# Expert weights in two column groups of 2048 and 1536, kept in a byte ring, in a decoder trunk

## The chip, the cores and the metric

One core of one Trainium2 chip runs the program. The metric is the device time of one execution in microseconds (us); lower is better. All inputs and outputs lie in HBM in float32.

## The reference, cut to what matters

Two decoder layers over 256 tokens of width 1024. Each has a token mixer, a cross attention into 256 memory tokens and a feed-forward part. The feed-forward part of the first layer is dense; that of the second routes each token to 2 of 8 experts:

```
logits = hf @ w_router                       # 256 x 8
topv, topi = top_k(logits, 2); wts = softmax(topv)
gate = sum over the two of one_hot(topi) * wts
for e in range(8):
    out += gate[:, e:e+1] * ((silu(hf @ wg[e]) * (hf @ wu[e])) @ wd[e])
```

wg[e] and wu[e] are 1024 x 3584, wd[e] is 3584 x 1024, so one expert has 44.04 MB of weights. A final RMSNorm follows.

## The kernel before, in words

**Two parts.** The trunk (both mixers, both attentions, the dense feed-forward) streams weights in units of 1 MB through six raw buffers, splits them into two float32r parts on ScalarE and VectorE and multiplies three times. The change does not touch that work, only where its buffers lie. The experts come last, on a plain float32 path: weights go from HBM to a slot and straight into TensorE as the moving operand.

**Visits.** Each expert is visited once (further visits would follow if an expert had more tokens than slots, which the code decides at run time; here there are eight visits). A visit holds up to 96 slots of tokens, as three groups (h) of 32; visits 1, 4 and 7 (LIGHT) take two groups, 64 slots. The gather (L1613) brings the visit's tokens into `he` by products with a selection matrix S. Gate and up products (gate_up, L1626) use 32 slot columns of `he` as the stationary operand and 256 weight columns as the moving one. Four column groups of the array (q = 0 to 3) work side by side, each on another quarter of the unit's columns and on another 32 partitions of PSUM. ScalarE applies silu (L868), VectorE multiplies with up (act_rows, L1253), TensorE transposes the result (act_t_, L1647), ScalarE copies it to SBUF as `aT` (L880), and the down products (L1660) sum into PSUM banks 4 and 5 over the whole visit. In the next visit the sum is evacuated by y_hi and y_lo (L855, L1227) and added to the tokens by the scatter (L1680, two products for each of four pieces) and add_piece (L1241). ST_AFTER places the slot products (L1705), which turn S into the rows that the next scatter needs; VectorE's slot_rows (L1248) copies them.

**Units.** The 3584 columns are four groups of 1024, 1024, 1024 and 512. A gate or up unit is 256 rows of one group: 2 rows of 4 KB to a partition. In the last group, gate and up share four units ("both"), each loaded by two DMAs of 512 KB with runs of 2 KB. A down unit is 256 rows of wd, again 2 rows of 4 KB to a partition. A visit has 42 units of 1 MB (BODY). Their order (`order`, L297 to L316) is gate, up, and then the down products of the group before.

**Slots.** The units go round 21 slots of 8 KB per partition (MR, L247), which lie over buffers that the trunk has finished with. The first 21 loads wait for the trunk to leave each place (L429 to L449); after that a load waits until the unit 21 places earlier is used (slot_wait, L418). All loads are issued by SyncE, in order, on one queue.

**PSUM.** Gate has banks 0 and 1, up 2 and 3, the down sums 4 and 5; scatter, slot products and transposes share 6 and 7. Where TensorE changes between products on 32 columns of the array and products on 128 (transposes, scatter, slot products, gather), T_AFTER, SCATTER_AFTER and ST_AFTER (L322 to L324) say after which unit.

Of the kernel before, what the change touches and what calls it, by code (L numbers as in the profile page):

```python
# [20 lines left out]
F32 = mybir.dt.float32  # L21
# [6 lines left out]
P = 128  # L28
# [4 lines left out]
MR = 21  # L33
# [14 lines left out]
def trunk(nc, a, out):  # L48
# [10 lines left out]
    NJ = DFE // C  # L59
    BODY = 6 * NJ  # L60
# [8 lines left out]
    assert NT == 2 and KD == 8 and NG == 4 and DEPTH == 2 and FH % P == 0 and BODY % MR == 0  # L69
# [63 lines left out]
    raw = [place(f"raw{i}", [P, UNIT], F32) for i in range(RAW)]  # L133
    whi = [place(f"whi{i}", [P, UNIT], F32R) for i in range(SPL)]
    wlo = [place(f"wlo{i}", [P, UNIT], F32R) for i in range(SPL)]
    x = place("x_res", [P, NT, D], F32)
    Ah = place("a_hi", [P, KD, SEQ], F32R)
    Al = place("a_lo", [P, KD, SEQ], F32R)
    Bh = place("b_hi", [P, KD, SEQ], F32R)
    Bl = place("b_lo", [P, KD, SEQ], F32R)  # L140
# [3 lines left out]
    vv = place("v_tok", [P, NT, D], F32)  # L144
    moe_top = at["top"]
    gT = place("gatesT", [P, 2 * KD, SEQ], F32)
    sc = at["top"]
    at["top"] += 32768
    ident = place("ident", [P, P], F32)
# [38 lines left out]
    hg = place("h_tok", [P, NT, D], F32, sc + 8192)  # L188
    m0 = moe_top + 8192

    def moe(name, shape, dt, region):
# [14 lines left out]
    silu_t = moe("silu_tmp", [P, SG * 256], F32, work)  # L206
    act_t = moe("act_tok", [P, SG * 256], F32, work)
# [34 lines left out]
    aT = [place("actT", [P, 2 * SG, P], F32, place_of["mem_lo"]), place("actT_end", [P, 2 * SG, P], F32, place_of["mem_lo"] + 4096)]  # L242
    gfin = place("g_final_rows", [P, D], F32, moe_top)

    SPLITS = [place_of[f"{w}{(U0 - SPL + i) % SPL}"] for i in range(SPL) for w in ("whi", "wlo")]
    RAWS = [place_of[f"raw{(U0 + i) % RAW}"] for i in range(RAW)]
    slots = [moe_top, place_of["b_hi"], place_of["b_lo"], sc + 24576] + RAWS[:4] + [  # L247
        place_of["kT"], place_of["v_tok"], sc + 16384] + RAWS[4:] + SPLITS + [place_of["a_lo"], sc]
    assert len(slots) == MR
    slot_t = [place(f"slot{i}", [P, UNIT], F32, where) for i, where in enumerate(slots)]  # L250

    def moe_raw(i):
        return slot_t[i % MR][:]
# [11 lines left out]
    with contextlib.ExitStack() as ctx:  # L265
# [4 lines left out]
        moe_loaded = [ctx.enter_context(nc.semaphore(f"moe_loaded{i}")) for i in range(MR)]  # L270
# [26 lines left out]
        GROUPS = [(j, min(2, NJ - j)) for j in range(0, NJ, 2)]  # L297
        GATE, UP, DOWN, order = [0] * len(GROUPS), [0] * len(GROUPS), [0] * len(GROUPS), []

        def add_group(w, g, first):  # L300
            first[g] = len(order)
            for part in range(2 * GROUPS[g][1]):
                order.append((w, g, part))

        for g in range(len(GROUPS)):
            if GROUPS[g][1] == 2:
                add_group("gate", g, GATE)
                add_group("up", g, UP)
            else:
                GATE[g] = UP[g] = len(order)  # L310
                for part in range(4):
                    order.append(("both", g, part))
            if g:
                add_group("down", g - 1, DOWN)
        add_group("down", len(GROUPS) - 1, DOWN)
        assert len(order) == BODY  # L316

        GATE_END = [GATE[g] + 4 for g in range(len(GROUPS))]
        UP_END = [UP[g] + 4 for g in range(len(GROUPS))]  # L320
        LOADS = [32 if w == "both" else 16 for w, _, _ in order]
# [3 lines left out]
        NG4 = len(GROUPS)  # L325
# [9 lines left out]
        def landed(i, v):  # L335

            m = i % MR
            return every(v, LOADS[m] + LOADS[m + MR], LOADS[i] + (LOADS[m] if i >= MR else 0))

        def y_piece(g, q):  # L340

            return ps[q * QP:(q + 1) * QP, 4:6, :].rearrange("p a b -> p (a b)")[:, g * 256:(g + 1) * 256]
# [9 lines left out]
        with nc.Block() as block:  # L352
# [3 lines left out]
            def _(sp):  # L356
# [39 lines left out]
                def load_expert_unit(i, e):  # L396
                    t = moe_raw(i)
                    w, g, part = order[i]
                    j, n = GROUPS[g]
                    if w == "both":  # L400
                        k = 2 * part
                        dst = t.rearrange("p (k h n) -> p k h n", k=2, h=2)
                        for h, name in enumerate(("w_e_gate", "w_e_up")):
                            src = a[name][0][bass.ds(e, 1), k * P:(k + 2) * P, j * C:(j + 1) * C]
                            sp.dma_start(dst[:, :, h, :], src.rearrange("e (k p) n -> p (e k) n", p=P)
                                         ).then_inc(moe_loaded[i % MR], 16)
                        return
                    if w == "down":
                        k, kk = 4 * j + 2 * part, 2
                        src = a["w_e_down"][0][bass.ds(e, 1), k * P:(k + kk) * P, :]  # L410
                    else:
                        kk = 2
                        k = kk * part
                        src = a["w_e_" + w][0][bass.ds(e, 1), k * P:(k + kk) * P, j * C:(j + n) * C]
                    dst = t.rearrange("p (k n) -> p k n", k=kk)
                    sp.dma_start(dst, src.rearrange("e (k p) n -> p (e k) n", p=P)).then_inc(moe_loaded[i % MR], 16)

                def slot_wait(i, v):  # L418

                    n = i - MR  # L420
                    sp.wait_ge(s["unit_used"], every(v, BODY, U0 + n + 1))

                def load(e, v):
                    for i in range(BODY):
                        slot_wait(i, v)
                        load_expert_unit(i, e)

                for i in range(MR):  # L429
                    if i == 1:  # L430

                        sp.wait_ge(s["unit_used"], mix_start[-1])
                    elif 4 <= i < 8:

                        sp.wait_ge(s["lo_ready"], U0 - RAW + i - 4 + 1)
                    elif i == 8:

                        sp.wait_ge(s["scores_done"], NH * DEPTH)
                    elif i == 9:

                        sp.wait_ge(s["o_done"], NH * DEPTH)
                    elif 11 <= i < 7 + RAW:
                        sp.wait_ge(s["lo_ready"], U0 - RAW + i - 7 + 1)
                    elif 7 + RAW <= i < 7 + RAW + 2 * SPL:
                        sp.wait_ge(s["unit_used"], U0 - SPL + (i - 7 - RAW) // 2 + 1)
# [1381 lines left out]
```

## Time and profile before

| | |
|---|---|
| median of 3 runs | 1585.14 us (1584.75 to 1585.96) |
| the profiled execution, its own time | 1584.88 us |
| its span, first to last instruction | 1583.2 us |
| granted TensorE clock, mean | 0.997 of full speed |
| busy: TensorE, VectorE, ScalarE | 99%, 32%, 26% |
| read from HBM | 475.61 MB |
| first product of the experts | 720.45 us into the span |
| first and last visit begin | 720.45 and 1487.18 us |

Engines are PE (TensorE matmul), PEld (its weight loads), DVE (VectorE), ACT (ScalarE), SPq (SyncE's queue). Times of a timeline are microseconds from the first instruction; "x192" counts instructions; a bracket gives the idle time of the engine before the row and what ended it, where "issue" is time in which it waited for nothing that the profile shows.
### The profile page before, as it was taken

What the parts mean: (1) busy time and instruction counts of PE and PEld (TensorE: products, weight loads), DVE (VectorE), ACT (ScalarE), POOL (GpSimd) and SP (SyncE); (2) the same over time, 40 slices, a digit from 0 to 9 for tenths busy, and PEclk for the clock granted to TensorE, in tenths of its full rate; (3) what the DMA queues carried; (4) which work ended last, traced back from release to release, by engine and by line L of the source; (5) the groups of instructions that cost most, each with busy time, mean ns of one, the idle gap of its engine ahead of it and who ended that gap; (6) DMA issues with size and microseconds to landing.
All of it is one profiled execution on the core that took longest, in us unless ns stands there. A gap on an engine that the chain in (4) does not pass through costs nothing. (4 is left out here: it accounts for less than half of the span.)

```text
span 1583.2 us, 42366 instructions
## 1 busy us (share of the span) xinstructions
PE 1564.0 (99%) x19703; PEld 1186.4 (75%) x19703; DVE 498.8 (32%) x563; ACT 412.2 (26%) x502; POOL 33.5 (2%) x119
## 2 busy tenths in 40 slices
PE   8999999999999999999999999999999999999996
PEld 8999898998989998986656566666565656655654
DVE  5554656455456646543002010020020100100202
ACT  5444464443445444531001010010010100100102
POOL 1000000000000000103000000000000000000000
PEclk9999999999999999999999999999999999999998
DMA  9655643556466555778999999999999999999995
GB/s 352 189 183 171 213 160 121 168 179 205 160 209 187 182 180 190 283 282 310 372 395 362 402 408 404 405 408 398 408 408 388 407 408 391 407 403 396 408 391 219
DMA packets 164693, 479.41 MB, mean 303 GB/s; under 512 B 9028, under 2 KB 14244, under 8 KB 164516
## 3 DMA queue, kind: packets, MB, share of 16 engines
q1 hardware_dynamic: 164516, 476.69, 80.7%
q8 instruction: 155, 2.54, 0.7%
q14 instruction: 22, 0.18, 0.0%
HBM read 475.61 MB, written 1.05 MB: 301 GB/s over the span
## 5 line engine op out<-in xcount | busy, mean ns | idle before, releaser
L1642 PE MATMUL ps<-slot,h_slots 128*32 128x256 f32 x9408 | 523.7, 380 | 0.0
L1642 PEld LDWEIGHTS ps<-slot,h_slots 128*32 128x32 f32 x9408 | 299.8, 110 | 205.3 <-issue 13.0
L930 DVE TENSOR_TENSOR wlo<-raw,whi 128x2048 fp32r<-128x2048 f32 (+1 forms) x116 | 259.0, 2236 | 208.1 <-ACT whi L602 208.1
L1337 PE MATMUL ps<-a_hi,whi 128*128 128x256 f32 x992 | 281.4, 284 | 0.0
L1337 PE MATMUL ps<-a_hi,wlo 128*128 128x256 f32 x992 | 280.7, 283 | 0.0
L1337 PE MATMUL ps<-a_lo,whi 128*128 128x256 f32 x992 | 280.7, 283 | 0.0
L602 ACT ACTIVATE whi<-raw 128x2048 fp32r<-128x2048 f32 (+1 forms) x116 | 216.7, 1869 | 162.9 <-PE ps L1337 104.6
L1674 PE MATMUL ps<-slot,actT 128*32 128x256 f32 x4032 | 223.6, 379 | 0.0
L1674 PEld LDWEIGHTS ps<-slot,actT 128*32 128x32 f32 x4032 | 130.2, 110 | 86.5 <-issue 1.3
L1337 PEld LDWEIGHTS ps<-a_lo,whi 128*128 128x128 f32 x992 | 190.4, 192 | 0.1
L1337 PEld LDWEIGHTS ps<-a_hi,whi 128*128 128x128 f32 x992 | 190.4, 192 | 0.1
L1337 PEld LDWEIGHTS ps<-a_hi,wlo 128*128 128x128 f32 x992 | 190.4, 192 | 0.0
L1260 DVE TENSOR_TENSOR act_tok<-silu_tmp,ps 128x768 f32<-128x768 f32 (+3 forms) x32 | 27.4, 856 | 493.5 <-PE ps L1642 341.9
L602 ACT ACTIVATE actT<-ps 128x768 f32<-128x768 f32 (+1 forms) x24 | 17.5, 731 | 565.4 <-PE ps L1657 565.4
L1246 DVE TENSOR_TENSOR x_res<-x_res,ps 128x512 f32<-128x512 f32 x32 | 21.3, 686 | 96.7 <-PE ps L1684 96.7
L1357 PE MATMUL ps<-whi,a_hi 128*128 128x512 f32 x128 | 50.7, 396 | 1.1 <-DVE a_lo L935 1.1
L1357 PE MATMUL ps<-wlo,a_hi 128*128 128x512 f32 x128 | 49.9, 389 | 0.0
L1357 PE MATMUL ps<-whi,a_lo 128*128 128x512 f32 x128 | 49.8, 389 | 0.0
L877 ACT ACTIVATE silu_tmp<-ps 128x768 f32<-128x768 f32 (+3 forms) x32 | 23.2, 726 | 74.9 <-PE ps L1642 74.9
L1674 PE MATMUL ps<-slot,actT_end 128*32 128x256 f32 x672 | 38.1, 380 | 0.6 <-DMA slot<-in_w_e_down 0.6
L1337 PE MATMUL ps<-mem_hi,whi 128*128 128x256 f32 x128 | 36.5, 285 | 0.0
L1337 PE MATMUL ps<-b_hi,whi 128*128 128x256 f32 x128 | 36.2, 283 | 0.0
(245 smaller groups left out, 1361.3 us busy)
## 6 DMA issues: line engine op xcount, KB each, us to landing
slot<-in_w_e_down SPq DMA_DIRECT2D x112, 1024.0 KB, 17.9
slot<-in_w_e_gate SPq DMA_DIRECT2D x96, 1024.0 KB, 18.6
slot<-in_w_e_up SPq DMA_DIRECT2D x96, 1024.0 KB, 18.7
raw<-in_w_in SPq DMA_DIRECT2D x32, 1024.0 KB, 5.5
slot<-in_w_e_gate SPq DMA_DIRECT2D x32, 512.0 KB, 8.5
slot<-in_w_e_up SPq DMA_DIRECT2D x32, 512.0 KB, 12.0
raw<-in_w_xk SPq DMA_DIRECT2D x8, 1024.0 KB, 5.2
raw<-in_w_xv SPq DMA_DIRECT2D x8, 1024.0 KB, 5.2
```

The lines of the kernel that those rows point to most:

```text
L602: return act.activation(dst, src, ACT.Copy, scale=scale)
L877: act.activation(silu_t[to, 0:w], ps[of, 0:2, :].rearrange("p a b -> p (a b)")[:, 0:w], ACT.Silu).then_inc(s["silu_ready"], 1)
L930: dve.tensor_tensor(wlo[n % SPL][:, 0:size], raw[n % RAW][:, 0:size], whi[n % SPL][:, 0:size].bitcast(F32), ALU.subtract).then_inc(s["lo_r ...
L1246: dve.tensor_tensor(xs, xs, bank(6 + n % 2), ALU.add).then_inc(s["xadd_done"], 1)
L1260: dve.tensor_tensor(act_t[of, 0:w], silu_t[of, 0:w], ps[of, b0:b0 + 2, :].rearrange("p a b -> p (a b)")[:, 0:w], ALU.mult).then_inc(s["act ...
L1337: ins = pe.matmul(o[:, d, :], w[wi][:, k, d * P:(d + 1) * P], xs[xi][:, k0 + k, :], start=first and d % 2 == 0, stop=last, skip_group_chec ...
L1357: ins = pe.matmul(o[:, t, 0:nn], xs[xi][:, k0 + k, t * P:(t + 1) * P], w[wi][:, k, :], start=j == 0 and k == 0 and n == 0, stop=j == n_uni ...
L1642: ins = pe.matmul(o[q * QP:(q + 1) * QP, h * n:(h + 1) * n], he[:, kt, h * QP:(h + 1) * QP], w[:, k, q * n:(q + 1) * n], start=kt == 0 and ...
L1674: ins = pe.matmul(o[q * QP:(q + 1) * QP, h * 256:(h + 1) * 256], lhs, w[:, k, q * 256:(q + 1) * 256], start=g == 0 and f == 0 and h % 2 == ...
```

## The change

- The 3584 columns become **two groups** of 2048 and 1536 (WIDE = 512 and 384 columns for each of the four column groups of the array). A product takes 512 or 384 weight columns.
- A gate or up unit is one k-tile of 128 rows: one run of 8 KB (1 MB in all) or 6 KB (768 KB) for a partition. A down unit has two consecutive rows to a partition (8 KB, 1 MB) in the first group and three (12 KB, 1.5 MB) in the second. A visit has 44 units: 28 of 1 MB or more and 16 of 768 KB.
- Since partition p of a down unit now holds consecutive rows of wd, the activations are permuted to match: silu reads PSUM as "(c b) -> b c" and writes `act_t`, and VectorE multiplies in place with the same order.
- The slots become a **ring of 168 KB** per partition in two halves, 22 units each (TURN); a load waits for the last unit of the other half that its bytes cover.
- PSUM: gate has banks 0 to 2, up 3 to 5, the down sums 6 and 7. Transposes use the up banks, the gather banks 3 and 4, the slot products bank 5, the scatter 3, 4, 6 and 7.
- Order of a visit on TensorE: 8 gate, 8 up, 4 gate of group 1, 2 down, 4 gate, 8 up, 6 down, 4 down. The scatter follows unit 2 in one stretch, the slot products unit 7, the transposes units 17 and 35, the gather unit 42.

```diff
-    slots = [moe_top, place_of["b_hi"], place_of["b_lo"], sc + 24576] + RAWS[:4] + [
-        place_of["kT"], place_of["v_tok"], sc + 16384] + RAWS[4:] + SPLITS + [place_of["a_lo"], sc]
+    order = []
+    order += [("gate", 0, k) for k in range(KD)] + [("up", 0, k) for k in range(KD)]
+    order += [("gate", 1, k) for k in range(4)] + [("down", 0, k) for k in range(2)]
+    TURN = len(order)
+    order += [("gate", 1, k) for k in range(4, KD)] + [("up", 1, k) for k in range(KD)]
+    order += [("down", 0, k) for k in range(2, 8)] + [("down", 1, k) for k in range(4)]
+    BODY = len(order)
...
+    def words(i):
+
+        w, g, _ = order[i]
+        return (2 * D, WIDE[1] // P * D)[g] if w == "down" else 4 * WIDE[g]
...
+    def covered(i):
+
+        other = range(TURN, BODY) if i < TURN else range(TURN)
+        return max(n for n in other if span[n][0] < span[i][1])
...
-        T_AFTER = [GATE[g + 1] + 3 for g in range(len(GROUPS) - 2)] + [GATE[-1] + 1, DOWN[-1] - 2]
-        SCATTER_AFTER = (GATE[0] + 3, GATE[0] + 3, UP[0] + 1, UP[0] + 2)
-        ST_AFTER = GATE[1] + 1
+        T_AFTER = (end_of("up", 0) + 1, end_of("up", 1) + 1)
+        SCATTER_AFTER, SCATTER_BANKS = 2, (3, 4, 6, 7)
+        ST_AFTER = first_of("up", 0) - 1
+        GATHER_AFTER = BODY - 2
...
+                    if w == "down":
+                        r, n = WIDE[g] // P, words(i) // D
+                        q, part = divmod(k, r // n)
+                        r0 = 4 * WIDE[0] * g + q * WIDE[g]
+                        src = a["w_e_down"][0][bass.ds(e, 1), r0:r0 + WIDE[g], :].rearrange("e (p r) n -> p (e r) n", r=r)
+                        src = src[:, part * n:(part + 1) * n, :]
...
+                        src = a["w_e_" + w][0][bass.ds(e, 1), k * P:(k + 1) * P, c0:c0 + 4 * WIDE[g]].rearrange("e p n -> p e n")
...
+                def ring_wait(i, v):
+
+                    n = covered(i) - (BODY if i < TURN else 0)
+                    sp.wait_ge(s["unit_used"], every(v, BODY, U0 + n + 1))
...
-                    elif i == MR - 1:
-
-                        sp.wait_ge(s["hg_ready"], NT)
...
+                    elif block == 20:
+                        sp.wait_ge(s["unit_used"], U0)
...
-                    act.activation(silu_t[to, 0:w], ps[of, 0:2, :].rearrange("p a b -> p (a b)")[:, 0:w], ACT.Silu
+                    act.activation(act_t[:, 0:n_groups * n].rearrange("p (h b c) -> p h b c", h=n_groups, c=P),
+                                   ps[:, 0:n_groups, 0:n].rearrange("p h (c b) -> p h b c", c=P), ACT.Silu
                                    ).then_inc(s["silu_ready"], 1)
...
-                dve.memset(ps[:, 4:6, :], 0.0)
-                dve.memset(ST[:].bitcast(F32), 0.0).then_inc(s["zero_done"], 1)
+                dve.memset(ST[:].bitcast(F32), 0.0)
...
+                    rows_ = act_t[:, 0:n_groups * n].rearrange("p (h b c) -> p h b c", h=n_groups, c=P)
+                    dve.tensor_tensor(rows_, rows_, ps[:, 3:3 + n_groups, 0:n].rearrange("p h (c b) -> p h b c", c=P),
                                       ALU.mult).then_inc(s["act_ready"], 1)
...
+                dve.memset(ps[:, 6:8, :], 0.0).then_inc(s["zero_done"], 1)
                 gathered(0)
...
+                    if k == 0 and w_name == "gate" and g:
+                        pe.wait_ge(s["silu_ready"], every(v, NG2, g))
+                    elif k == 0 and w_name == "up" and g == 0:
                         pe.wait_ge(s["xadd_done"], every(v, 4, 4))
                         pe.wait_ge(s["st_ready"], every(v, 1, 1))
+                    elif k == 0 and w_name == "up":
+                        pe.wait_ge(s["actT_ready"], every(v, NG2, g))
...
+                    for h in range(n_groups):
+                        for q in range(4):
+                            ins = pe.matmul(ps[q * QP:(q + 1) * QP, b0 + h, 0:n], he[:, k, h * QP:(h + 1) * QP],
+                                            w[:, q * n:(q + 1) * n], start=k == 0, stop=k == KD - 1, skip_group_check=True)
...
+                def scatter(v):
+
+                    pe.wait_ge(s["he1_ready"], every(v, 1, 1))
+                    pe.wait_ge(s["y_ready"], every(v, 2, 2))
+                    for n, b in enumerate(SCATTER_BANKS):
...
                     for i in range(BODY):
                         (down if order[i][0] == "down" else gate_up)(i, v, n_groups)
-                        for n in range(4):
-                            if i == SCATTER_AFTER[n]:
...
+                        if i == SCATTER_AFTER:
+                            scatter(v)
                         if i == ST_AFTER:
...
+                            slot_t(v)
```

## Rows read from the trace of the kernel before

**Rows 1.** The page: its span, and TensorE's and VectorE's busy time

```profile
span 1583.2 us, 42366 instructions
PE 1564.0 (99%) x19703; PEld 1186.4 (75%) x19703; DVE 498.8 (32%) x563; ACT 412.2 (26%) x502; POOL 33.5 (2%) x119
```

**Rows 2.** The waits, 700 to 1583 us: total, times, longest; all that name TensorE and DMA

```profile
PE ps L1674 <- DMA slot<-in_w_e_down: 0.6, 1, 0.6
```

**Rows 3.** Timeline of TensorE's weight loads, visit 0 and the start of visit 1

```profile
720.45 10.09 PEld L1642 LDWEIGHTS ps<-slot,h_slots 128*32 128x32 f32 x192
...
750.07 4.91 PEld L1642 LDWEIGHTS ps<-slot,h_slots 128*32 128x32 f32 x96
755.39 0.64 PEld L1657 LDWEIGHTS ps<-ident,act_tok 128*128 128x128 f32 x6 [0.41 <-issue]
756.19 10.09 PEld L1642 LDWEIGHTS ps<-slot,h_slots 128*32 128x32 f32 x192 [0.17 <-issue]
766.36 10.27 PEld L1674 LDWEIGHTS ps<-slot,actT 128*32 128x32 f32 x192
776.72 10.27 PEld L1642 LDWEIGHTS ps<-slot,h_slots 128*32 128x32 f32 x192
...
840.44 6.82 PEld L1642 LDWEIGHTS ps<-slot,h_slots 128*32 128x32 f32 x128
847.67 0.19 PEld L1684 LDWEIGHTS ps<-y_hi,sel_slot 128*128 128x128 f32 x1 [0.41 <-issue]
...
848.79 3.18 PEld L1642 LDWEIGHTS ps<-slot,h_slots 128*32 128x32 f32 x64 [0.37 <-issue]
852.38 0.19 PEld L1684 LDWEIGHTS ps<-y_hi,sel_slot 128*128 128x128 f32 x1 [0.41 <-issue]
...
853.05 1.45 PEld L1642 LDWEIGHTS ps<-slot,h_slots 128*32 128x32 f32 x32 [0.36 <-issue]
```

**Rows 4.** The weight queue, 860 to 1560 us: packets, MB, share of 16 engines

```profile
q1 hardware_dynamic: 80246, 279.98, 101.4%
```

**Rows 5.** The same queue, 1330 to 1410 us (80 us, 4 KB runs alone)

```profile
q1 hardware_dynamic: 8408, 32.41, 101.6%
```

**Rows 6.** The same queue, 1202 to 1208 us (6 us, 2 KB runs among them)

```profile
q1 hardware_dynamic: 725, 1.84, 92.0%
```

**Rows 7.** Timeline of TensorE's weight loads in the last visit

```profile
1508.35 3.18 PEld L1642 LDWEIGHTS ps<-slot,h_slots 128*32 128x32 f32 x64
1511.94 0.42 PEld L1657 LDWEIGHTS ps<-ident,act_tok 128*128 128x128 f32 x4 [0.41 <-issue]
1512.52 6.63 PEld L1642 LDWEIGHTS ps<-slot,h_slots 128*32 128x32 f32 x128 [0.17 <-issue]
...
1565.57 1.48 PEld L1674 LDWEIGHTS ps<-slot,actT_end 128*32 128x32 f32 x32 [1.01 <-issue]
```

**Rows 8.** Timeline of VectorE after the slot products of visit 0

```profile
750.18 0.42 DVE L1250 CAST sel_slot<-ps 128x256 fp32r<-128x256 f32 x1 [4.90 <-PE ps L1712]
750.52 0.15 DVE L1251 COPY gate_slot<-ps 128x1 f32<-128x1 f32 x1
```

**Rows 9.** Timeline of VectorE as y is evacuated at the start of visit 1

```profile
840.90 2.61 DVE L1233 COPY y_slots<-ps 32x256 f32<-32x256 f32 x6 [4.79 <-PE ps L1674]
843.99 1.41 DVE L1238 SCALAR_TENSOR_TENSOR y_lo<-y_slots,gate_slot,y_hi 96x512 fp32r<-96x512 f32 x2 [0.48 <-ACT y_hi L602]
```

**Rows 10.** Groups by shape, 700 to 1583 us: busy, mean ns, idle before, releaser

```profile
L1260 DVE TENSOR_TENSOR act_tok<-silu_tmp,ps 128x768 f32<-128x768 f32 x15 | 14.3, 955 | 244.5 <-PE ps L1642 244.5
L602 ACT ACTIVATE actT<-ps 128x768 f32<-128x768 f32 x15 | 12.2, 811 | 401.2 <-PE ps L1657 401.2
L1260 DVE TENSOR_TENSOR act_tok<-silu_tmp,ps 128x512 f32<-128x512 f32 x9 | 6.2, 688 | 97.4 <-PE ps L1642 97.4
```

**Rows 11.** The weight queue in the trunk, 300 to 400 us (100 us)

```profile
q1 hardware_dynamic: 10209, 18.73, 58.0%
```

More of the change, by code:

```diff
@@ L58, in trunk @@
     C = 512
-    NJ = DFE // C
-    BODY = 6 * NJ
+    WIDE = (512, 384)
     OVER = ROUNDS * NE
@@ L143, in trunk @@
     kT = place("kT", [P, KD, SEQ], F32)
-    vv = place("v_tok", [P, NT, D], F32)
     moe_top = at["top"]
     gT = place("gatesT", [P, 2 * KD, SEQ], F32)
+    Bh = place("b_hi", [P, KD, SEQ], F32R)
+    Bl = place("b_lo", [P, KD, SEQ], F32R)
+    for u in range(U0 - RAW, U0 - 2):
+        raw[u % RAW] = place(f"raw{u % RAW}", [P, UNIT], F32)
     sc = at["top"]
     at["top"] += 32768
+    vv = place("v_tok", [P, NT, D], F32)
+    for u in range(U0 - 2, U0):
+        raw[u % RAW] = place(f"raw{u % RAW}", [P, UNIT], F32)
+    for u in range(U0 - SPL, U0):
+        whi[u % SPL] = place(f"whi{u % SPL}", [P, UNIT], F32R)
+        wlo[u % SPL] = place(f"wlo{u % SPL}", [P, UNIT], F32R)
+    Al = place("a_lo", [P, KD, SEQ], F32R)
+    ring, ring_end = moe_top + 8192, at["top"]
     ident = place("ident", [P, P], F32)
@@ L241, in trunk, with first_of, end_of @@
     yl = place("y_lo", [P, D], F32R, place_of["mem_hi"] + 4096)
[L242 to L246, printed above, removed]
-    slots = [moe_top, place_of["b_hi"], place_of["b_lo"], sc + 24576] + RAWS[:4] + [
-        place_of["kT"], place_of["v_tok"], sc + 16384] + RAWS[4:] + SPLITS + [place_of["a_lo"], sc]
[L249 to L253, printed above, removed]
+    aT = [place("actT", [P, SG * WIDE[0] // P, P], F32, place_of["mem_lo"]),
+          place("actT_end", [P, SG * WIDE[1] // P, P], F32, m0)]
+    gfin = place("g_final_rows", [P, D], F32, ring)
+    order = []
[5 more added lines that the diff above has]
+    BODY = len(order)
+    def first_of(w, g):
+        return order.index((w, g, 0))
+    def end_of(w, g):
+        return max(i for i, o in enumerate(order) if o[:2] == (w, g)) + 1
+    def words(i):
+        w, g, _ = order[i]
+        return (2 * D, WIDE[1] // P * D)[g] if w == "down" else 4 * WIDE[g]
+    span, unit_t = [], []
+    for i in range(BODY):
+        b0 = 0 if i in (0, TURN) else span[-1][1]
+        span.append((b0, b0 + 4 * words(i)))
+        assert ring + span[-1][1] <= ring_end
+        unit_t.append(place(f"unit{i}", [P, words(i)], F32, ring + b0))
+    assert span[TURN - 1][1] == span[-1][1] == ring_end - ring
+    def covered(i):
+        other = range(TURN, BODY) if i < TURN else range(TURN)
+        return max(n for n in other if span[n][0] < span[i][1])
     names = """const_loaded mem_loaded mem_t1_loaded x_loaded wpg_loaded wrt_loaded gbc_loaded setup_done
@@ L295, in cols @@
             return ap[:, :, c * C:(c + 1) * C]
[L297 to L321, printed above, removed]
-        T_AFTER = [GATE[g + 1] + 3 for g in range(len(GROUPS) - 2)] + [GATE[-1] + 1, DOWN[-1] - 2]
-        SCATTER_AFTER = (GATE[0] + 3, GATE[0] + 3, UP[0] + 1, UP[0] + 2)
-        ST_AFTER = GATE[1] + 1
-        NG4 = len(GROUPS)
+        NG2 = len(WIDE)
+        T_AFTER = (end_of("up", 0) + 1, end_of("up", 1) + 1)
+        SCATTER_AFTER, SCATTER_BANKS = 2, (3, 4, 6, 7)
+        ST_AFTER = first_of("up", 0) - 1
+        GATHER_AFTER = BODY - 2
         def every(v, per, n):
@@ L1634, in gate_up @@
[L1634 to L1644 removed]
+                    w_name, g, k = order[i]
```

229 lines of the change are left out of this document (89 added, 140 removed).

## The prediction

> **What bounds the kernel now.** I read the page first. TensorE is busy in 99% of the span and no other engine in more than 32% [rows 1], which says little by itself, since ends of matmuls are modelled. The list of waits says more: over the whole expert stage, from 720.45 us on, TensorE is seen waiting for a transfer once, for 0.6 us [rows 2]. The timeline of its weight loads then gives the rate. 192 loads run from 766.36 to 776.72, so one record (half of a product of the source, which is two records) costs 53.96 ns, or 215.8 ns for the four column groups that run together [rows 3]. At the granted full clock that is 518 cycles for 256 columns. If a record streams two cycles to a column, 512 of them are streaming and 2.5 ns are left for each four.
>
> With that rate the whole first visit closes: 2016 records (108.8 us), four rounds of transposes, three interruptions by the scatter, one by the slot products, one gather; it lasts from 720.45 to 840.44 [rows 3]. So **TensorE paces the stage**. The visits with two groups of slots issue 1344 records.
>
> The transfers are close behind. From 860 to 1560 the weight queue moved 279.98 MB, 400 GB/s [rows 4]; in a stretch of 4 KB runs it moves 405 [rows 5], and where the 2 KB runs of the last column group pass, 307 [rows 6]. Only the end shows the tie: the last unit found TensorE idle for 1.01 us [rows 7], the one place where the stock of loaded units had run out.
>
> **The change, part by part.** All prices are per visit, for a visit of three groups of slots (five) and of two (three).
>
> *Wide products.* The gate and up products go from 256 columns to 512 and 384. Columns streamed stay the same. Records fall from 1344 to 768 (896 to 512), so 144 (96) fewer groups of four, at 2.5 ns each: **-0.36 (-0.24) us**. The page "TensorEngine Tiling (Array Packing)" of the Trainium skill, section "Instruction Overhead", gives about 60 cycles of overhead to each matmul; at the full clock that is an estimate of 25 ns on each of the 4032 records removed, 101 us in all, against 2.5 us by the row. The row decides here; the other is a rival below.
>
> *Transposes.* A round of six costs what 750.07 to 756.19 holds beyond 96 records: 6.12 - 5.18 = 0.94 us [rows 3]. A round of four costs 4.17 - 3.45 = 0.72, from 1508.35 to 1512.52 [rows 7]. That is 0.28 for switching and 0.11 for each. Now four rounds (3.76; 2.88). After: two rounds, 12 and 9 transposes (8 and 6): 1.60 + 1.27 = 2.87 (1.16 + 0.94 = 2.10). **-0.89 (-0.78).**
>
> *Scatter.* One piece between products costs 4.26 - 3.45 = 0.81 us (848.79 to 853.05); the stretch of two pieces is 1.12 long where that of one is 0.67 [rows 3], so another piece adds 0.45. Three interruptions become one of four pieces: 2 x (0.81 - 0.45) = **-0.72**.
>
> *A wait is added.* The slot products now stand right before the first up product, which waits for VectorE to have copied their result, because they share a bank. Before, TensorE resumed at 750.07 and VectorE finished only at 750.52 + 0.15 [rows 3, 8]. Allowing 0.1 for the restart, the bubble is 0.70: **+0.70**. Everything on TensorE queues behind it. It can't be below zero, and above I allow 1.5.
>
> *The earlier scatter.* It waits for the evacuated y after three units instead of four. After a full visit, y was complete at 843.99 + 1.41 = 845.40, that is 4.96 after the first load of 840.44 [rows 3, 9]. Three new units take 7.7 us with three groups, but 48 x 107.3 ns = 5.15 with two, plus 0.1 of draining. Nothing is paid, with 0.3 us to spare in three visits; if y is late the price is the lateness, three times.
>
> *Activations.* VectorE's product over 768 elements takes 955 ns and over 512 takes 688 [rows 10], so 1536 elements take 1.75 us. It must be over before the transposes two units later, 3.87 us (2.58) after the last up product. ScalarE's copy grows the same way, 811 ns at 768 to 1.45, beside the next two gate units. The permuted read (a stride of 16 bytes) is nowhere in this trace: its bounds are no cost and twice the time (3.4 us). Both fit in the cover, the second barely, so I take nothing. If the cover fails, the transposes wait, and everything behind them. Silu reads under eight up units and cannot matter.
>
> *Setup.* The clearing of the y banks moves behind the rank products on VectorE (0.9 us, while VectorE awaits the gather), and the last ring slot no longer waits for the token rows. The first unit starts when it did: nothing.
>
> Sum: -0.36 - 0.89 - 0.72 + 0.70 = -1.27 in a full visit, -0.24 - 0.78 - 0.72 + 0.70 = -1.04 in a light one. 5 x 1.27 + 3 x 1.04 = 9.5, and the 1.0 us idle at the end goes too if transfers keep up: **-10.5 us**.
>
> *Do they keep up?* The last unit would have to land about 11.5 us sooner: its three rows take 2.6 us of products, and TensorE is 9 to 10 ahead. 279.98 MB in 688.5 us is 407 GB/s [rows 4]. Flat 4 KB runs give 405 [rows 5]; the short fall of 0.4% is about 3 us. The new runs are 6 to 12 KB. A packet took 1300 us / 8408 = 155 ns at a mean of 3855 B [rows 5] and 928 / 10209 = 91 ns at 1835 B [rows 11]; drawn on, 8 KB would take 292 ns, 449 GB/s. So the supply lies between 405 and 449 if longer runs do no harm. I take 415; anything over 407 gives the same time. The ring holds as much as before (21 MB), and releases at most one unit later.
>
> The profiled execution took 1584.88, its span 1583.2; less 10.5 is 1574.4, and since it stood 0.26 below the median of the runs shown, **1574.5** for the median.
>
> **The rivals.**
>
> *Transfers take over mildly (0.12).* If runs are cut at 4 KB, or 6 KB ones into 4 and 2, the supply stays at 402 to 405: 3 to 8 us of the gain are lost, 1577 to 1582. Against: the mean is now pulled down by 2 KB runs, which vanish.
>
> *Transfers take over badly; slower (0.13).* Sixteen of the 44 loads, 28.6% of the bytes, are 768 KB instead of 1 MB. The only smaller loads now, 512 KB each, are where the rate sinks to 307 [rows 6]. The Trainium skill speaks against such units: "DMA: Bandwidth & Descriptors", section "Rules for kernel authors", wants at least 1 MiB per DMA for full bandwidth. In rows: if these bytes move at r and the rest at 405, the mean falls under today's 400 from r = 388 down. At r = 350, about halfway to the 2 KB stretch, the mean is 388, 280 MB take 722 us instead of 700, and the time is about 1605. Against: those 512 KB loads also had 2 KB runs and came in pairs, which explains the dip as well. A run's start stride of 16 KB in the down weights could do the same.
>
> *The waits take it back (0.09).* If the bubble is 1.5 us, y is 1 us late in the light visits, and the strided reads overrun their cover by 0.5 in each visit, that is 6.4 + 3 + 4 = 13 us: about 1588. It decides from 1.3 us of extra waiting per visit. With half of it, 1581.
>
> *Records carry more overhead than the rate shows (0.04).* At 25 ns for each of 4032 records TensorE would save 101 us, but supply would bind at once: 280 MB at 415 GB/s takes 675 us where it took 700, so 1560 at best. Against: 215.8 ns leave no room for it.
>
> **How the numbers follow.** My own case has 0.62 and spans 1571 to 1577 (bubble 0.4 to 1.2, rounds 20% off). The range 1570.5 to 1583.5 takes in the mild transfer case and half of the waits' case and leaves out the bad transfer case, the rest of the waits and the overhead case, some 0.2. This kernel's measurement tells 0.2%, 3 us, from no change. Faster by more than that (below 1582): 0.62 + 0.11 + 0.04 + 0.02 = 0.79; within: 0.07; slower: 0.14.
>
> **What the changed profile would show.** Right: weight loads 107 ns apart (mean) in the first group and 80.6 in the second; two rounds of transposes with 12 and 9; one scatter of four pieces; an idle of TensorE's loads of 0.6 to 0.8 us after each slot stretch, released by VectorE's gate_slot; full visits of 118.7 us and light ones of 82; GB/s that falls below the cap in full visits, because the ring is full; no wait for a transfer. Wrong: waits for slots behind DMA in several visits (transfers bind), VectorE's act_tok over 3 us, or records that differ from 107 and 80.6 ns.

## The result, and the profile after

The changed kernel takes 1574.33 us (median of 4 runs, 1573.99 to 1574.77), the kernel before 1584.95 beside it on the same chip: a ratio of 0.9933 (95% interval 0.9922 to 0.9945), 10.6 us less. The prediction was 1574.5.

The page of the kernel after; its first lines answer to [rows 1], and the packets and MB of the instruction queue, before 155 and 2.54, matter further down:

```profile
span 1572.9 us, 34011 instructions
PE 1550.6 (99%) x15650; PEld 1070.5 (68%) x15650; DVE 492.3 (31%) x547; ACT 404.7 (26%) x470; POOL 33.3 (2%) x119
...
q8 instruction: 123, 2.02, 0.5%
```

The list of waits has no transfer for TensorE at all (before, one of 0.6 us [rows 2]). The timeline of TensorE's weight loads, visit 0 and what follows, answers to [rows 3]:

```profile
720.39 0.16 PEld L1630 LDWEIGHTS ps<-unit,h_slots 128*32 128x32 f32 x8
720.84 0.13 PEld L1630 LDWEIGHTS ps<-unit,h_slots 128*32 128x32 f32 x4 [0.30 <-issue]
721.27 0.13 PEld L1630 LDWEIGHTS ps<-unit,h_slots 128*32 128x32 f32 x4 [0.30 <-issue]
...
728.25 0.19 PEld L1668 LDWEIGHTS ps<-y_hi,sel_slot 128*128 128x128 f32 x1 [0.84 <-issue]
...
730.29 0.16 PEld L1630 LDWEIGHTS ps<-unit,h_slots 128*32 128x32 f32 x8 [0.35 <-issue]
...
743.30 0.20 PEld L1676 LDWEIGHTS ps<-ident,sel_tok 128*128 128x128 f32 x2 [0.84 <-issue]
743.47 0.53 PEld L1678 LDWEIGHTS ps<-gate_of_visit,sel_tok 128*128 128x128 f32 x4
744.68 0.19 PEld L1630 LDWEIGHTS ps<-unit,h_slots 128*32 128x32 f32 x8 [0.68 <-issue]
...
769.32 1.29 PEld L1639 LDWEIGHTS ps<-ident,act_tok 128*128 128x128 f32 x12 [0.62 <-issue]
770.78 0.16 PEld L1630 LDWEIGHTS ps<-unit,h_slots 128*32 128x32 f32 x8 [0.17 <-issue]
...
808.37 0.96 PEld L1639 LDWEIGHTS ps<-ident,act_tok 128*128 128x128 f32 x9 [0.41 <-issue]
809.50 10.09 PEld L1655 LDWEIGHTS ps<-unit,actT 128*32 128x32 f32 x192 [0.17 <-issue]
...
839.12 0.35 PEld L1630 LDWEIGHTS ps<-unit,h_slots 128*32 128x32 f32 x8
...
844.59 0.19 PEld L1668 LDWEIGHTS ps<-y_hi,sel_slot 128*128 128x128 f32 x1 [0.84 <-issue]
...
921.12 0.34 PEld L1630 LDWEIGHTS ps<-unit,h_slots 128*32 128x32 f32 x8
...
1546.52 10.27 PEld L1655 LDWEIGHTS ps<-unit,actT_end 128*32 128x32 f32 x192
```

Read it from the top. Loads come in fours, 0.43 us apart: the array holds four column groups at work, and the next four wait for 512 columns to pass. The idle of 0.30 before each four costs nothing, since loading overlaps the products. Visit 0 lasts from 720.39 to 839.12, 118.73 us, where it lasted 119.99; the light visit 1 from 839.12 to 921.12, 82.00, where it lasted 83.03 (840.44 to 923.47). Five times 1.26 and three times 1.03 make 9.4 us. The last row is one unbroken run of 192 loads, where before TensorE had idled 1.01 us for its last unit [rows 7]. Together 10.4 us, beside the 10.3 by which the span is shorter.

VectorE after the slot products and at the next visit's start ([rows 8, 9]):

```profile
744.12 0.42 DVE L1238 CAST sel_slot<-ps 128x256 fp32r<-128x256 f32 x1 [12.62 <-PE ps L1678]
744.46 0.15 DVE L1239 COPY gate_slot<-ps 128x1 f32<-128x1 f32 x1
...
839.58 2.61 DVE L1221 COPY y_slots<-ps 32x256 f32<-32x256 f32 x6 [3.50 <-PE ps L1655]
842.67 1.41 DVE L1226 SCALAR_TENSOR_TENSOR y_lo<-y_slots,gate_slot,y_hi 96x512 fp32r<-96x512 f32 x2 [0.49 <-ACT y_hi L597]
```

The second row ends at 744.61, and TensorE loads for its first up product at 744.68: this is the added wait. The last row ends at 844.08, 0.5 us ahead of the scatter at 844.59, so the earlier scatter waits for nothing even in a light visit.

Groups by shape for the activations ([rows 10]):

```profile
L1247 DVE TENSOR_TENSOR act_tok<-act_tok,ps 128x1536 f32<-128x1536 f32 x5 | 8.8, 1755 | 104.8 <-PE ps L1630 104.8
L870 ACT ACTIVATE act_tok<-ps 128x1536 f32<-128x1536 f32 x5 | 7.3, 1452 | 95.7 <-PE ps L1630 95.7
L597 ACT ACTIVATE actT<-ps 128x1536 f32<-128x1536 f32 x5 | 7.3, 1451 | 129.9 <-PE ps L1639 129.9
```

Silu reads PSUM in steps of 16 bytes and takes 1452 ns; ScalarE's copy of as many elements reads it in order and takes 1451.

The weight queue, 860 to 1540 us and then 980 to 1080 (packets, MB, share of 16 engines), answers to [rows 4, 5]:

```profile
q1 hardware_dynamic: 40248, 280.93, 100.1%
q1 hardware_dynamic: 6002, 41.74, 100.6%
```

413 GB/s over the whole stretch, 417 in the second, where the queue was busy throughout. In the first stretch 4477 of the packets have under 512 bytes; the others have 7.8 KB on average, as the runs of 6, 8 and 12 KB of a visit have (44.04 MB in 5632 runs). In the second stretch the trace has packets of 6144, 8192 and 12288 bytes and, besides them, only some of 4 bytes, so the runs pass whole.

### The profile page after: what moved, and what is told of

Same layout as the page of the kernel before. It is cut to its first block and busy times, and to the rows that moved or that the text cites. A ratio compares the mean times of both kernels' runs of the same rounds, so it can differ in the third digit from the quotient of the medians.

```text
span 1572.9 us, 34011 instructions
## 1 busy us (share of the span) xinstructions
PE 1550.6 (99%) x15650; PEld 1070.5 (68%) x15650; DVE 492.3 (31%) x547; ACT 404.7 (26%) x470; POOL 33.3 (2%) x119
## 3 DMA queue, kind: packets, MB, share of 16 engines
q8 instruction: 123, 2.02, 0.5%
## 5 line engine op out<-in xcount | busy, mean ns | idle before, releaser
L1630 PE MATMUL ps<-unit,h_slots 128*32 128x384 f32 (+1 forms) x5376 | 513.1, 539 | 5.0 <-issue 5.0
L1630 PEld LDWEIGHTS ps<-unit,h_slots 128*32 128x32 f32 x5376 | 183.4, 110 | 312.9 <-issue 310.4
L1655 PE MATMUL ps<-unit,actT 128*32 128x256 f32 x2688 | 149.6, 379 | 0.0
L1247 DVE TENSOR_TENSOR act_tok<-act_tok,ps 128x1536 f32<-128x1536 f32 (+3 forms) x16 | 22.1, 1380 | 396.5 <-PE ps L1630 396.5
L1655 PEld LDWEIGHTS ps<-unit,actT 128*32 128x32 f32 x2688 | 86.5, 110 | 61.1 <-issue 7.5
L1655 PE MATMUL ps<-unit,actT_end 128*32 128x256 f32 x2016 | 111.7, 379 | 0.0
L1655 PEld LDWEIGHTS ps<-unit,actT_end 128*32 128x32 f32 x2016 | 64.8, 110 | 42.9
L870 ACT ACTIVATE act_tok<-ps 128x1536 f32<-128x1536 f32 (+3 forms) x16 | 18.4, 1151 | 241.0 <-PE ps L1630 241.0
L597 ACT ACTIVATE actT<-ps 128x1536 f32<-128x1536 f32 (+1 forms) x8 | 10.3, 1291 | 183.3 <-PE ps L1639 183.3
L597 ACT ACTIVATE actT_end<-ps 128x1152 f32<-128x1152 f32 (+1 forms) x8 | 8.1, 1012 | 144.4 <-PE ps L1639 144.4
```

What stands on the lines that cost most here:

```text
L597: return act.activation(dst, src, ACT.Copy, scale=scale)
L870: act.activation(act_t[:, 0:n_groups * n].rearrange("p (h b c) -> p h b c", h=n_groups, c=P), ps[:, 0:n_groups, 0:n].rearrange("p h (c b) ...
L1247: dve.tensor_tensor(rows_, rows_, ps[:, 3:3 + n_groups, 0:n].rearrange("p h (c b) -> p h b c", c=P), ALU.mult).then_inc(s["act_ready"], 1)
L1630: ins = pe.matmul(ps[q * QP:(q + 1) * QP, b0 + h, 0:n], he[:, k, h * QP:(h + 1) * QP], w[:, q * n:(q + 1) * n], start=k == 0, stop=k == KD ...
L1655: ins = pe.matmul(o[q * QP:(q + 1) * QP, h * 256:(h + 1) * 256], lhs, w[:, k, q * 256:(q + 1) * 256], start=g == 0 and part == 0 and k == ...
```

## The experiments

Two questions were open. First, whether the parts of the working (products, switches, scatter, slot wait) are each what the sum says, or whether errors cancelled. Second, what the transfers had to do with it: the rate rose from 400 to 413 GB/s, and the time could have followed that alone. Each kernel is compared with the kernel before on its own chip; all are edits of the changed kernel, one excepted. Where a difference from the changed kernel is given, it is taken across chips, on which the kernel before agrees within 0.2 us (1584.75 to 1584.96).

**Slot products two units earlier.** They then have two gate units behind them, and nothing waits for the bank they use.

```diff
-        ST_AFTER = first_of("up", 0) - 1
+        ST_AFTER = first_of("up", 0) - 3
```

> The changed kernel, with the slot products after unit 5 instead of unit 7, so that VectorE has two more units of time before the first up product. If TensorE paces the stage, the bubble measured in the changed kernel (744.68 - 743.84 = 0.84 us from the last slot product to the next load, 0.18 in the kernel before) goes in all eight visits: 8 x 0.67 = 5.3 us, so about 1569. If the gain of the change came from the faster loads and the supply still set the pace, nothing moves: 1574.

Measured: 1569.2 us (1568.87 to 1569.27), ratio 0.9903 (0.9888 to 0.9918). The timeline of its weight loads:

```profile
738.32 0.20 PEld L1676 LDWEIGHTS ps<-ident,sel_tok 128*128 128x128 f32 x2 [0.84 <-issue]
738.48 0.53 PEld L1678 LDWEIGHTS ps<-gate_of_visit,sel_tok 128*128 128x128 f32 x4
739.02 0.16 PEld L1630 LDWEIGHTS ps<-unit,h_slots 128*32 128x32 f32 x8
```

The idle of 0.68 us behind the slot products is gone, and the time fell by 5.1 us, a little under eight times that. So a wait of TensorE returns to the time in full, with the rate of the transfers left as it was: TensorE paces this kernel.

**The scatter in three stretches again.** After units 2, 4 and 5: three stretches, as before the change.

```diff
-        SCATTER_AFTER, SCATTER_BANKS = 2, (3, 4, 6, 7)
+        SCATTER_AFTER, SCATTER_BANKS = (2, 2, 4, 5), (3, 4, 6, 7)
```

> The changed kernel, with the scatter in three stretches again (two pieces after unit 2, one after unit 4, one after unit 5). If TensorE paces the stage, two more interruptions cost 2 x (0.81 - 0.45) = 0.72 us in each of eight visits: +5.8 us, about 1580. Between wide products, where the step from the last product to the switch is 0.52 us instead of 0.31, the same holds, since the 0.21 more is streaming. If supply paces: nothing.

Measured: 1580.15 us (1579.23 to 1581.37, 9 runs), ratio 0.9972 (0.9962 to 0.9982): 5.8 us for sixteen more interruptions, 0.36 each, as [rows 3] say for a small piece joined to another (0.81 - 0.45).

**The products cut in half.** Every gate and up product by two of half the columns, 256 and 192.

```diff
-                        for q in range(4):
-                            ins = pe.matmul(ps[q * QP:(q + 1) * QP, b0 + h, 0:n], he[:, k, h * QP:(h + 1) * QP],
...
+                        for c in range(2):
+                            for q in range(4):
+                                ins = pe.matmul(ps[q * QP:(q + 1) * QP, b0 + h, c * m:(c + 1) * m], he[:, k, h * QP:(h + 1) * QP],
```

> The changed kernel, with every gate and up product cut in two of half the columns (256 and 192), as narrow as before the change. Records of these products double from 5376 to 10752, that is 1344 more groups of four. If a group costs 2.5 ns on top of its streaming, +3.4 us: 1577.7. If each record carries 25 ns of its own, 5376 x 25 = +134 us, or some tens of us if part of that hides beside other column groups. If the supply sets the pace, nothing moves.

Measured: 1596.54 us (1594.27 to 1599.22), ratio 1.0077 (1.0063 to 1.009). This is 22.2 us over the changed kernel where 3.4 were expected. Its weight loads in the 192-column products of visit 0:

```profile
792.10 5.14 PEld L1632 LDWEIGHTS ps<-unit,h_slots 128*32 128x32 f32 x128 [0.89 <-issue]
798.03 5.14 PEld L1632 LDWEIGHTS ps<-unit,h_slots 128*32 128x32 f32 x128 [0.79 <-issue]
804.23 1.61 PEld L1632 LDWEIGHTS ps<-unit,h_slots 128*32 128x32 f32 x42 [1.06 <-issue]
```

and what the list of waits (700 to 1600 us) has for them:

```profile
PEld ps L1632 <- issue: 24.9, 43, 1.2
```

In these rows TensorE stops for about a microsecond after each 128 loads, and no semaphore, transfer or other engine is named. (The 24.9 us of the list also hold other idle, such as the slot wait of 0.68 us in each visit.) It does not stop at every block of 128: a full visit has six blocks of the 192-column loads and stops at two or three of them. Over the whole expert stage there are 23 such stops of 0.2 to 1.3 us, five of them in the down products right behind, 19.6 us in all. With the 3.4 us expected that is 23.0, and 22.2 were measured.

128 loads and 128 products are 256 instructions. The instruction queue moved 2.02 MB in 123 packets in the kernel after, 16.4 KB each, and that kernel has 31300 loads and products, 254 to a packet. So a block of instructions is one packet, and the trace shows that it comes too late: the packets of the rows above end at 790.71, 796.72 and 802.97 us, and the loads go on 1.3 to 1.4 us later, at 792.10, 798.03 and 804.23. Each of the 21 stops over 0.4 us ends 1.3 to 1.6 us after the end of an instruction packet. In the 256-column gate and up products no such stop occurs: there 128 pairs last 6.9 us, here 5.2.

**Only the first group cut in half, and in quarters.** These tell the late blocks from a cost of each cut. The edit is the one above with m = n // 2 or n // 4 where g == 0, and m = n where g == 1.

> The changed kernel, but the products of the first group are cut in two again (256 columns where 512 were); those of the second group keep 384 columns. It adds 16 units x 3 groups of slots x 2 records = 96 groups of four records to a full visit and 64 to a light one, at 2.5 ns each: 0.24 and 0.16 us, 1.7 us in all. Theory A (the time lost when both groups were cut lay in the 192-column products alone, because there a load and its product last 40.5 ns and TensorE runs out of instructions): 1576.0 us, between 1574.5 and 1578, with no idle of 0.4 us or more within the up and gate stretches. Theory B (a cut costs time wherever it is made, in proportion to the cuts: 22 us for both groups, just as many cuts in each): 11 us, about 1585.

> The changed kernel, but the products of the first group are cut in four (128 columns). A full visit then has 1536 loads with their products in this group, a light one 1024, each with 26.7 ns of streaming. Theory A (delivery of instructions: 128 pairs of load and product per block, and a block comes in about 6.05 us at best, as the 192-column stretches suggest, so 47.3 ns for a pair): each full visit gains (47.3 - 27.3) x 1536 = 30.7 us, each light one 20.5, 215 us in all, about 1790 (1720 to 1800), in idle gaps that recur about every 6 us between stretches of even 27 ns. Theory B (columns and 2.5 ns for each four records alone): 5.0 us, about 1579. Theory C (a weight load can't follow another in under some 30 to 50 ns): a time anywhere between 1579 and 1790, but with the loads evenly spaced and no recurring gaps.

Measured: 1576.29 us (1576.03 to 1576.56, 5 runs) in halves, ratio 0.9947 (0.9933 to 0.996), 2.0 us over the changed kernel, where the price of 2.5 ns for each four records gives 1.7; in quarters 1700.38 us (1696.86 and 1703.89), ratio 1.073 (1.0708 to 1.0752). The weight loads of the kernel with quarters:

```profile
749.48 6.98 PEld L1632 LDWEIGHTS ps<-unit,h_slots 128*32 128x32 f32 x256 [1.26 <-issue]
758.60 3.49 PEld L1632 LDWEIGHTS ps<-unit,h_slots 128*32 128x32 f32 x128 [2.13 <-issue]
763.43 3.49 PEld L1632 LDWEIGHTS ps<-unit,h_slots 128*32 128x32 f32 x128 [1.34 <-issue]
767.16 3.49 PEld L1632 LDWEIGHTS ps<-unit,h_slots 128*32 128x32 f32 x128 [0.25 <-issue]
770.90 1.90 PEld L1632 LDWEIGHTS ps<-unit,h_slots 128*32 128x32 f32 x71 [0.25 <-issue]
```

Each burst has 128 loads or twice that (the last row is cut off by the end of these products), evenly 27.3 ns apart, so a load can follow another that fast, and 128 columns keep the price of 2.5 ns for each four. Between the bursts TensorE stands for 0.25 to 2.13 us; over the expert stage it stands at 61 places for 0.2 to 3.5 us, 98.5 us in all. Each of the 52 stops over 0.4 us ends 1.2 to 1.6 us after the end of an instruction packet: TensorE runs out of instructions at the end of a block. The expected 1790 was too much: I had taken 6.05 us for a block at best, and here blocks start 4.8, 3.7 and 3.7 us apart (758.60, 763.43, 767.16, 770.90). In the two stretches that I compared they are quicker where the weights move slower: those rows lie in a stretch at 310 GB/s (749 to 771 us); from 1240 to 1260, at 374, blocks start 4.6 and 6.2 us apart. That fits an instruction queue that shares the DMA engines with the weights; it was not tried apart.

Stops and record overhead (98.5 + 5.0 us) leave 19 of the 122.5 us by which the profiled execution is longer. The clock accounts for most of that. Two rows from further on:

```profile
1252.77 3.49 PEld L1632 LDWEIGHTS ps<-unit,h_slots 128*32 128x32 f32 x128 [1.09 <-issue]
1258.99 5.16 PEld L1632 LDWEIGHTS ps<-unit,h_slots 128*32 128x32 f32 x128 [2.73 <-issue]
```

The same 128 loads take 5.16 us instead of 3.49, and the granted clock from 1255 to 1265 us is 0.83 in the mean. It is at half (1.2 GHz) in ten stretches between 891 and 1625 us, 37 us in all, which costs up to 19 us. Each of them follows a stop of 2.4 to 3.0 us, though other stops as long left the clock at full. The kernels before and after keep it full through all their expert products.

**Shorter runs, the same loads.** The same 44 loads per visit, each as runs of 4 KB (3 KB for 768 KB units): the unit holds half the columns of two k-tiles instead of all columns of one.

```diff
-                        src = a["w_e_" + w][0][bass.ds(e, 1), k * P:(k + 1) * P, c0:c0 + 4 * WIDE[g]].rearrange("e p n -> p e n")
+                        k0, m = k // 2 * 2, 4 * WIDE[g] // 2
+                        c0 += k % 2 * m
+                        src = a["w_e_" + w][0][bass.ds(e, 1), k0 * P:(k0 + 2) * P, c0:c0 + m].rearrange("e (k p) n -> p (e k) n", p=P)
```

> The changed kernel with the same 44 DMAs of the same sizes, but runs of 4 KB (3 KB in the second group's gate and up units, 4 KB in the down units); the numbers land in other places, so the experts' products are made of other numbers. The supply should fall from the measured 419 to about 405 GB/s. From 860 us on some 282 MB are to be moved: 696 us, so the last unit lands near 1556 where TensorE wants it at 1554.3: a tie, 1574 to 1578. If runs of 4 KB in 768 KB units were as bad as the 307 GB/s stretch, 1640 and more.

Measured: 1581.81 us (1581.17 to 1582.24), ratio 0.9979 (0.997 to 0.9988): 7.5 us of the gain are gone. Its weight queue from 980 to 1080 us, the one wait for transfers in the list, and the end of its loading in stretches (us; then PE, PEld, DVE, ACT, POOL busy, clock, share of the DMA engines, GB/s):

```profile
q1 hardware_dynamic: 11276, 40.46, 102.0%
```

```profile
PE ps L1657 <- DMA unit<-in_w_e_down: 6.0, 6, 1.9
```

```profile
1540.00:1552.00 12.00, 8.92 (x153) 5.17 (x155) 0.00 (x0) 0.81 (x1) 0.00 (x0) 1.00 1.02 408
1552.00:1556.00 4.00, 2.96 (x56) 1.90 (x52) 0.00 (x0) 0.00 (x0) 0.00 (x0) 1.00 0.89 351
1556.00:1560.00 4.00, 3.07 (x60) 1.93 (x53) 0.00 (x0) 0.00 (x0) 0.00 (x0) 1.00 0.51 209
1560.00:1564.00 4.00, 3.05 (x60) 1.95 (x56) 0.00 (x0) 0.00 (x0) 0.00 (x0) 1.00 0.27 109
```

At 405 GB/s TensorE waits nowhere until 1543 us; then the stock of loaded units is gone, and it waits for each of the last ones. The expectation (1574 to 1578) took the rate as constant to the last byte. It isn't: from 1552 us on fewer and fewer of the sixteen engines are at work (shares of 0.89, 0.51 and 0.27), while each packet of 4 KB takes as long as before (162 ns, 164 from 980 to 1080 us), and the last 2.7 MB take 12 us. The kernel before ended in the same way (217 GB/s from 1558 to 1566).

**Runs of 2 KB and 1.5 KB.** In gate and up units four pieces for each partition; the down units have rows of 4 KB.

```diff
+                        k0, m = k // 4 * 4, 4 * WIDE[g] // 4
+                        c0 += k % 4 * m
+                        src = a["w_e_" + w][0][bass.ds(e, 1), k0 * P:(k0 + 4) * P, c0:c0 + m].rearrange("e (k p) n -> p (e k) n", p=P)
```

> The same with runs of 2 KB in the first group's gate and up units and 1.5 KB in the second's (DMA sizes unchanged, two thirds of the bytes). Here the supply must set the pace. If short runs alone pull the rate down and a 2 KB packet takes 91 ns or less, the mean is 370 to 394 GB/s: 282 MB take 716 to 762 us, the end moves by 21 to 67 us: 1595 to 1640. If the dips to 307 GB/s belong to 2 KB runs as such, two thirds at 307 give a mean of 335: about 1720.

Measured: 1610.53 us (1610.38 to 1612.03), ratio 1.0162 (1.0147 to 1.0178). The weight queue from 980 to 1080 us, and one of five such waits:

```profile
q1 hardware_dynamic: 17263, 38.97, 103.7%
```

```profile
PE ps L1657 <- DMA unit<-in_w_e_down: 17.4, 19, 1.9
```

390 GB/s, and TensorE now runs out of units in two of the light visits, which use them fastest: in visit 4 (1209 to 1244 us; the visit lasts 94.2 us instead of 82.0) and in the last (from 1520 us on). In the full visits it waits for none.

**Smaller loads.** Each gate or up unit by two DMAs, each down unit row by row: 384 to 512 KB each, runs of 3 to 4 KB.

```diff
+                        m = 2 * WIDE[g]
+                        for j in range(2):
+                            sp.dma_start(dst[:, :, j * m:(j + 1) * m], src[:, :, j * m:(j + 1) * m]).then_inc(moe_loaded[i], 16)
```

> The changed kernel, every unit loaded by two or three DMAs of 384 or 512 KB with runs of 3 or 4 KB (numbers unchanged). If small DMAs are harmless and only the run counts, this equals the kernel with 4 KB runs in 44 DMAs: 1574 to 1578. If small DMAs were what pulled the rate down to 307 GB/s in the kernel before, 280 MB take 900 us and the time passes 1750; half of that effect gives about 1660.

Measured: 1583.89 us (1582.27 to 1584.45), ratio 0.9989 (0.998 to 0.9999). The weight queue in the same stretch:

```profile
q1 hardware_dynamic: 11966, 40.47, 102.1%
```

The rate is that of the kernel with the large loads and 4 KB runs, 405 GB/s (40.47 MB against 40.46). Half the size for every load costs 2.1 us, run length the rest. The 2.1 us come at the end again: the waits of TensorE's products and loads for the last down units add up to 9.9 us in the list, against 6.0 above.

**The kernel before with even loads.** Its shared units come by one DMA of 1 MB with 4 KB runs instead of two of 512 KB with 2 KB.

```diff
-                        for h, name in enumerate(("w_e_gate", "w_e_up")):
-                            src = a[name][0][bass.ds(e, 1), k * P:(k + 2) * P, j * C:(j + 1) * C]
...
+                        src = a["w_e_gate"][0][bass.ds(e, 1), k * P:(k + 2) * P, (j - 1) * C:(j + 1) * C]
```

> The kernel before, but the four units that gate and up share are loaded by one DMA of 1 MB in runs of 4 KB (other columns of the gate weights, so the last group's products are made of other numbers; all else is as before). The dips to 307 GB/s go and the mean rate rises from 400 to 405. If TensorE paces the stage, only the idle at the end goes: -1.0 to -1.3 us, about 1584. If the supply had paced the kernel before, the 1.3% more rate over 700 us gives -8 to -9 us: 1576.

Measured: 1583.93 us (1583.28 to 1584.34), ratio 0.9994 (0.9985 to 1.0003), 0.8 us. Its weight queue, 860 to 1540 us:

```profile
q1 hardware_dynamic: 71044, 273.88, 101.1%
```

403 GB/s, and no wait for a transfer is left. The rate rose less than expected, by 0.6% over the same stretch (272.16 MB before) instead of 1.3%. Had the supply paced the kernel, that would still be worth some 4 us; the interval of the ratio reaches from 2.4 us faster to 0.5 us slower. So a faster supply by itself gives the kernel before no more than about its one idle at the end: the transfers did not pace it.

**A better version.** The slot products join the scatter, from visit 1 on, and the gather joins the second round of transposes (it uses the gate banks there): two switches fewer per visit, and no wait.

```diff
-        ST_AFTER = first_of("up", 0) - 1
-        GATHER_AFTER = BODY - 2
+        ST_AFTER = first_of("up", 0) - 3
+        GATHER_AFTER = T_AFTER[1]
...
-                        if i == ST_AFTER:
+                        if i == (ST_AFTER if isinstance(v, int) and v == 0 else SCATTER_AFTER):
```

> The changed kernel, with the slot products in the same stretch as the scatter (from visit 1 on; after unit 5 in visit 0) and the gather in the same stretch as the second round of transposes (banks 0 and 1 in place of 3 and 4). If TensorE paces the stage, the bubble goes (8 x 0.67 = 5.3 us) and 7 + 7 switches go at about 0.3 us each (4.2 us): about 1565. If the supply binds first, it stops earlier; at 419 GB/s it would allow 1560.

Measured: 1565.56 us (1565.34 to 1566.14), ratio 0.9877 (0.9862 to 0.9892); it beats both kernels. Its weight loads at the start of visit 1:

```profile
846.28 0.19 PEld L1669 LDWEIGHTS ps<-y_lo,sel_slot 128*128 128x128 f32 x1
846.51 0.37 PEld L1677 LDWEIGHTS ps<-ident,sel_tok 128*128 128x128 f32 x2
846.85 0.52 PEld L1679 LDWEIGHTS ps<-gate_of_visit,sel_tok 128*128 128x128 f32 x4
847.39 0.16 PEld L1631 LDWEIGHTS ps<-unit,h_slots 128*32 128x32 f32 x8
```

Scatter, slot products and the next unit follow without a stop. Of the 8.8 us under the changed kernel, 5.1 are the wait, as above; the rest, 3.7, is about 0.26 us for each of the fourteen switches, where 0.3 was expected.

## Why the prediction was right, point by point

**What bounds it.** That TensorE paces the stage was read from the rate of its weight loads and from the missing waits. It holds: taking away TensorE time gave it back one for one (slot products earlier, -5.1; scatter apart, +5.8), and supply alone gave 0.8 us, which is within the noise of no change.

**The terms, each against its row.**

| part, full visit | predicted | measured | from |
|---|---|---|---|
| wide products, ns for each four records | 2.5 | 107.3 and 80.6 ns for a record, as predicted; 2.0 us for the first group cut again (1.7) | timeline; first group in halves |
| round of 12 transposes | 1.60 us | 1.63 | 744.68 to 770.78, less 192 records at 107.3 ns and 48 at 80.6 |
| scatter, three stretches to one | -0.72 | -0.72 | 5.8 us / 8 |
| added wait | +0.70 | +0.68 (+0.64) | idle at 744.68 (5.1 us / 8) |
| earlier scatter | 0 | 0, 0.5 us spare | end of y_lo, 844.08 |
| activations, 1536 elements | 1.75 us, hidden | 1.755, hidden | groups by shape |
| full visit, light visit | 118.7, 82 | 118.73, 82.00 | weight loads |
| idle at the end | -1.0 | -1.0 | last visit |

The step that was bounded widest, the permuted read of PSUM (nothing to twice the time), came out at its lower end.

**The supply.** Here the outcome was right and the margin was thinner than the text made it. I took 415 GB/s between 405 and 449; the queue gives 417 when it isn't held up. The line drawn through two packet sizes erred: at 6955 bytes it gives 253 ns for a packet, and the row gives 1.006 x 1600 us / 6002 = 268. Both of its means held packets of 4 bytes (9 ns each) beside the real ones; by single sizes the traces have 88 ns for 2 KB, 164 for 4 KB and 314 for 8 KB, where the line gave 292. "Anything over 407 gives the same time" is not shown, since no run lies between 405 and 413; what lies under it costs more than I wrote. At 405 GB/s I priced the shortfall at about 3 us, and the kernel with 4 KB runs lost 7.5, because the queue empties at half its rate or less over the last 8 us. The change therefore has two parts that need each other. Fewer switches and interruptions make TensorE's work 10 us shorter; the longer runs, which nobody waits for, are what lets 7.5 of them reach the time.

**The rivals.** *Transfers mildly* did not happen, as packets of 6 KB pass whole; where I forced it, it cost what the rival said (1577 to 1582; measured 1581.8). *Transfers badly* falls by its cause: with 768 KB units the queue gives 417 GB/s, and with 384 to 512 KB ones 405, the same as large loads with equal runs. The Trainium skill, "DMA: Bandwidth & Descriptors", section "Rules for kernel authors", wants at least 1 MiB per DMA; here halving the loads costs 2.1 us in 1582. The dip to 307 GB/s [rows 6], on which I rested this rival, is neither small loads nor short runs alone (390 GB/s with 2 KB runs). It was also the lowest 6 us of all stretches with such runs. The kernel before has one visit's whole share of 2 KB runs between 980 and 1080 us as well, and there its queue moved 403 GB/s:

```profile
q1 hardware_dynamic: 11551, 40.35, 102.0%
```

What slowed some packets in the dip stays unexplained. *The waits* stayed at 0.68 us a visit. That rival needed 1.3 us on top of the 0.70 that the sum already held, and there was nothing on top. *Overhead of records* falls: at 128, 256, 384 and 512 columns each four records cost some 2.5 ns beyond their streaming. The rule of the Trainium skill, "TensorEngine Tiling (Array Packing)", section "Instruction Overhead", of some 60 cycles for each matmul, taken as time on top of the streaming, would have made the kernel with the first group in halves some 67 us slower (2688 more records at 25 ns, an estimate from the page); it was 2.0. Yet short products do have a price of another kind, which I had not thought of, below.

## What to carry to other kernels

To see which of two close resources paces a kernel, take the spacing of the work that can't be delayed (here weight loads: 216 ns for each four, with no gaps) and check that it closes a whole period to a tenth of a microsecond; then each added switch or wait can be priced from a row, and eight small terms add up to a forecast. Ask of the other resource not only whether its mean rate is enough, but how much stock is left at the end and how it drains: a supply 2% short of what was used (405 against 413 GB/s) cost nothing for 800 us and 7.5 us in the last 20. A sequence of short switches costs less when the pieces stand together, and a piece with a reader on another engine belongs ahead of work that doesn't need its bank.

## What the hardware showed that I had not expected

- **TensorE can run out of instructions.** With 40.5 ns for each pair of load and product it stops at some of the block ends, 128 pairs apart, for 0.2 to 1.3 us; with 27.3 ns at most of them, for 0.2 to 3.5. At 53.9 ns it stops only right behind a 192-column stretch. One packet of the instruction queue holds 256 instructions, and a stop ends 1.2 to 1.6 us after the end of a packet. So narrowing products below 256 columns cost far more here than their own overhead: 22 us for halving all, 126 us for quartering the first group, up to 19 of them by the lower clock that followed the longest stops.
- **A read of PSUM in steps of 16 bytes costs nothing**: silu over 1536 elements 1452 ns, the plain copy 1451; VectorE's product 1755, where the plain reads of before, drawn on, give 1756.
- **Run length sets the rate of a full queue**: 390 GB/s with runs of 1.5 to 4 KB, 405 with 3 to 4 KB, 417 with 6 to 12 KB, with little regard to the size of a load.
- **The queue drains unevenly**: in the kernel with 4 KB runs at 351, 209 and 109 GB/s in the last three stretches of 4 us, with 1.0 us and more of waiting for each of the last units, because fewer of the engines are at work and not because packets are slower.
